# A new opening for a kernel of four transformer layers: fewer rows first, statistics on VectorE, warm-up on a cleared block

## The reference

```python
def rmsnorm(x, g):
    y = xf * lax.rsqrt(jnp.mean(xf * xf, axis=-1, keepdims=True) + RMS_EPS)
    return (y * g.astype(jnp.float32)).astype(x.dtype)

# layer 0, even_mixer
z = rmsnorm(h, mix_norm_g[0]) @ w_in           # w_in: 1024 x 2048
gate_b, gate_c, val, pool_in = z[..., :512], z[..., 512:1024], z[..., 1024:1536], z[..., 1536:]
y_a = gate_b * causal_dwconv(gate_c * val, conv_w)
y_b = multiscale_pool(pool_in, pool_w, pool_scale)
h = h + jnp.concatenate([y_a, y_b], axis=-1) @ w_out
```

## Time and profile before

| what | value |
|---|---|
| median of 3 runs | 1239.06 us (1238.93 to 1239.44) |
| profiled execution | 1239.02 us, its span 1237.3 us |
| TensorE busy | 1222.6 us, 99% of the span |
| VectorE busy | 972.4 us, 79% |
| ScalarE busy | 703.6 us, 57% |
| GpSimd busy | 137.8 us, 11% |
| DMA | 265.78 MB, 215 GB/s on average, 323 GB/s in the first fortieth |

### The profile page before, as it was taken

The page is one execution under the profiler, slowest core; times in us unless marked ns, Lnnn a source line. Parts: engine busy times, 40 slices in busy tenths (PEclk is TensorE's granted clock), DMA queues, the critical chain, the costliest instruction groups (busy, mean ns, idle before and its releaser), DMA issues.

```text
span 1237.3 us, 18561 instructions
## 1 busy us (share of the span) xinstructions
PE 1222.6 (99%) x7005; PEld 1060.6 (86%) x7005; DVE 972.4 (79%) x1232; ACT 703.6 (57%) x1061; POOL 137.8 (11%) x253
## 2 busy tenths in 40 slices
PE   8999999999999999999999999999999999999998
PEld 7989888888778989998889888888878998888887
DVE  5867999977885888898788787997785888676564
ACT  6555555556565655555687566555664353755552
POOL 5000000010001111111132301220010010000000
PEclk9999999999999999999999999999999999999999
DMA  9746777765572798894132348997566488385550
GB/s 323 237 156 211 246 245 237 222 205 183 177 216 69 227 324 312 315 337 128 55 99 93 137 146 294 392 392 259 179 210 216 171 303 273 109 288 195 190 187 34
DMA packets 153777, 265.78 MB, mean 215 GB/s; under 512 B 6220, under 2 KB 110608, under 8 KB 153712
## 3 DMA queue, kind: packets, MB, share of 16 engines
q1 hardware_dynamic: 134560, 204.75, 49.0%
q0 software_dynamic: 18672, 59.67, 13.7%
q10 hardware_dynamic: 480, 0.49, 0.1%
HBM read 263.79 MB, written 1.09 MB: 214 GB/s over the span
## 4 chain that ended last, share of the span: by engine, by line
PE 85%; DVE 9%; ACT 3%; issue 2%; POOL 1%; DMA 1%; ACTq 0%; POOLq 0%; DVEq 0%
PE ps L1969 24%; PE ps L1949 17%; PE ps L1952 9%; PE ps L1935 4%; PE ps L1934 4%; PE ps L1933 4%; DVE w_lo L1150 3%; PE ps L2012 2%; PE ps L2014 2%; PE ps L2013 2%; PE ps L2076 2%; PE ps L1990 2%; PE ps L1992 2%; PE ps L1991 2%; PE ps L2078 2%
## 5 line engine op out<-in xcount | busy, mean ns | idle before, releaser
L1150 DVE TENSOR_TENSOR w_lo<-raw,w_hi 128x2048 fp32r<-128x2048 f32 (+3 forms) x211 | 433.8, 2070 | 31.6 <-ACT w_hi L589 31.3
L589 ACT ACTIVATE w_hi<-raw 128x2048 fp32r<-128x2048 f32 (+3 forms) x213 | 368.7, 1737 | 58.5 <-PE ps L1969 49.2
L1949 PE MATMUL ps<-xn,w_hi 128*128 128x512 f32 x976 | 243.9, 392 | 0.1
L1949 PEld LDWEIGHTS ps<-xn,w_hi 128*128 128x128 f32 x976 | 178.2, 188 | 34.6 <-issue 0.6
L1952 PEld LDWEIGHTS ps<-xn,w_lo 128*128 128x128 f32 x976 | 133.1, 190 | 9.6
L1952 PE MATMUL ps<-xn,w_lo 128*128 128x256 f32 x976 | 136.1, 282 | 0.0
L1969 PE MATMUL ps<-w_hi,a_hi 128*128 128x512 f32 x432 | 134.6, 393 | 0.2 <-DVE a_lo L1874 0.2
L1969 PE MATMUL ps<-w_lo,a_hi 128*128 128x512 f32 x432 | 133.5, 390 | 0.0
L1969 PE MATMUL ps<-w_hi,a_lo 128*128 128x512 f32 x432 | 133.2, 390 | 0.0
L670 ACT ACTIVATE work<-ps 128x512 f32<-128x512 f32 x61 | 36.3, 595 | 168.1 <-PE ps L1952 168.1
L1933 PE MATMUL ps<-xn,w_hi 128*128 128x256 f32 x432 | 122.6, 284 | 0.0
(11 more groups left out here) (370 smaller groups left out, 2006.8 us busy)
## 6 DMA issues: line engine op xcount, KB each, us to landing
raw<-in_ffn_w SPq DMA_DIRECT2D x64, 1024.0 KB, 5.6
side<-in_ada_w POOLq DMA_DIRECT2D x96, 512.0 KB, 6.0
raw<-in_ffn_w_in SPq DMA_DIRECT2D x40, 1024.0 KB, 5.2
raw<-in_ffn_w_out SPq DMA_DIRECT2D x32, 512.0 KB, 5.2
raw<-in_gm_w_in SPq DMA_DIRECT2D x16, 1024.0 KB, 6.0
raw<-in_od_w_in SPq DMA_DIRECT2D x12, 1024.0 KB, 5.6
raw<-in_gm_w_out SPq DMA_DIRECT2D x8, 1024.0 KB, 5.2
raw<-in_ev_w_in SPq DMA_DIRECT2D x7, 1024.0 KB, 12.9
```

The costliest lines, as they stand in the source:

```text
L589: nc.scalar.activation(w_hi[s][:, 0:w], raw[s][:, 0:w], ACT.Copy).then_inc(hi_done, 1)
L1150: nc.vector.tensor_tensor(w_lo[s][:, 0:w], raw[s][:, 0:w], w_hi[s][:, 0:w].bitcast(F32), ALU.subtract)\
L1949: nc.tensor.matmul(o, hi, xn[:, 512 * k:512 * k + 512], start=k == 0, stop=False)
```

## The change

Everything is in the opening, up to the first f tiles.

- Rows: ScalarE's queue loads only the 16 rows of mix_norm_g ahead (`first_rows`). The other 359 rows and the tail of the constants move to SyncE's queue, behind the loads of tiles T_EV to T_EV+3. They are turned after the first f tile, all three groups anew, and VectorE copies them behind the rest of T_EV+3.
- Loads: SyncE loads x's first half, the two parts of T_EV, x's second half, the two parts of T_EV+1, then the others. GpSimd's first side loads wait for `lo_done`.
- Statistics of x's first half: VectorE, with bn_stats and bn_aggr (mean squared plus variance), the power still on GpSimd. The squares of the second half stay with ScalarE, but stand between the second and the third part of the weights. VectorE scales half a row of the second half, GpSimd the other.
- Warm-up: 28 products on a block cleared by GpSimd, before any DMA has landed, then the transpose of the 16 rows, eight products on `ident`, x's transposes, four more products.
- Inputs: ScalarE writes `xn_hi` straight from PSUM, VectorE makes `xn_lo` out of PSUM with one scalar_tensor_tensor for each k. The second half of x is turned into other banks, by fours, ahead of k = 4 and k = 6.
- ScalarE runs one tiny Square first; one semaphore of the conv is merged into another.

```diff
-        first_rows = [x for x in row_pieces if x[0] == 0]
-        later_rows = [x for x in row_pieces if x[0]]
+        first_rows, later_rows = row_pieces[:1], row_pieces[1:]
+        N_FIRST = first_rows[0][2]
...
+        def turned(name, t, b):
+            if name == "ev":
+                c = (b % 2) * P + (S if t and b < 4 else 0)
+                return ps[((2, 3, 5, 6), (2, 3, 4, 7))[t][b // 2]][:, c:c + P]
+            return ps[bank_of(name, t, b // 4)][:, (b % 4) * P:(b % 4) * P + P]
+
+        warm = acc[:, 4, 0:P]
...
+            load_x(0)
+            load_part(T_EV, 0)
+            load_part(T_EV, 1)
+            load_x(1)
+            for m in range(2):
+                load_part(T_EV + 1, m)
+            for t in range(T_EV + 2, T_EV + 4):
+                load(t)
+            for r, p, m, src in later_rows:
+                sp.dma_start(stage[p:p + m, r, :], src).then_inc(in_later, 16)
+            sp.dma_start(cst[:, P:], I["consts"][:, P:C_ALL]).then_inc(in_later, 16)
+            for t in range(T_EV + 4, T_FFN0):
                 load(t)
...
-                    last = gain_op(xf[:, b, t * P:t * P + P], ps[bank_of("ev", t, b // 4)][:, (b % 4) * P:(b % 4) * P + P], ev_gain, None, b)
+                    last = gain_op(xn_hi3[:, b, t * P:t * P + P], turned("ev", t, b), ev_gain, None, b)
...
-            half_squares("ev", 0)
-            half_squares("ev", 1)
+            act.wait_ge(half_ready, 2)
+            nc.scalar.activation(rs[:, 39:40], half[:, 0:1], ACT.Square)
             for i in range(4):
+                if i == 2:
+                    half_squares("ev", 1)
                 split_part(T_EV + i // 2, i % 2)
...
             dve.wait_ge(in_h[0], 16)
+            for c in range(2):
+                last = nc.vector.bn_stats(st[:, 40 + 6 * c:46 + 6 * c], h[:, 0, 512 * c:512 * c + 512])
+            chain(last)
+            chain(nc.vector.bn_aggr(st[:, 4:6], st[:, 40:52]))
+            chain(nc.vector.tensor_scalar(rs[:, 0:1], st[:, 4:5], st[:, 4:5], EPS, ALU.mult, ALU.add))
+            nc.vector.tensor_tensor(rs[:, 0:1], rs[:, 0:1], st[:, 5:6], ALU.add).then_inc(first_stats, 1)
+            dve.wait_ge(vec_ps, 1)
+            nc.vector.tensor_copy(vec[:, 0:N_FIRST], ps[4][:, 0:N_FIRST]).then_inc(vec_ready, 1)
             half_scale("ev", 0)
...
+            def ev_rest(t, i):
+                dve.wait_ge(xf_ready, 4 * t + i + 1)
+                for b in (2 * i, 2 * i + 1):
+                    q = slice(t * P, t * P + P)
+                    last = nc.vector.scalar_tensor_tensor(xn_lo3[:, b, q], turned("ev", t, b), col("mix_norm_g", b),
+                                                          xn_hi3[:, b, q].bitcast(F32), ALU.mult, ALU.subtract)
+                last.then_inc(xn_ready, 1)
+
             for i in range(4):
                 split_part(T_EV + i // 2, i % 2)
-                take("ev", 0, (i,))
-            take("ev", 1)
-            dve.wait_ge(vec_ps, 2)
-            nc.vector.tensor_copy(vec[:, P:N_ROWS], ps[4][:, P:N_ROWS]).then_inc(vec_ready, 1)
+                if i == 2:
+                    dve.wait_ge(rstd_ready, 2)
+                    nc.vector.tensor_scalar(hs[:, 1, 0:512], h[:, 1, 0:512], rstd[:, 1:2], None, ALU.mult).then_inc(hs_ready, 1)
+                ev_rest(0, i)
+            for i in range(4):
+                ev_rest(1, i)
...
             split(T_EV + 2)
             split(T_EV + 3)
+            dve.wait_ge(vec_ps, 2)
+            nc.vector.tensor_copy(vec[:, N_FIRST:N_ROWS], ps[4][:, N_FIRST:N_ROWS]).then_inc(vec_ready, 1)
...
+                            if tt == 0 and name == "ev" and k in (4, 6):
+                                transposes(name, 1, (k // 2 - 2,))
+                            elif tt == 0 and k == 6:
                                 transposes(name, 1)
-                            if name == "ev" and tt == 1 and k == 0:
-                                later_vec_rows()
...
+            pe.wait_ge(half_ready, 2)
+            for _ in range(28):
+                nc.tensor.matmul(ps[7][:, 0:P], warm, warm, start=True, stop=True)
             pe.wait_ge(in_id, 16)
-            for _ in range(11):
+            pe.wait_ge(in_rows, 16)
+            nc.tensor.transpose(ps[4][:, 0:N_FIRST], stage[0:N_FIRST, 0, :], ident[0:N_FIRST, 0:N_FIRST]).then_inc(vec_ps, 1)
+            for _ in range(8):
                 nc.tensor.matmul(ps[7][:, 0:P], ident, ident, start=True, stop=True)
-            pe.wait_ge(in_rows, 16 * len(first_rows))
-            vec_rows(0).then_inc(vec_ps, 1)
             transposes("ev", 0)
-            for _ in range(7):
+            for _ in range(4):
                 nc.tensor.matmul(ps[7][:, 0:P], ident, ident, start=True, stop=True)
...
+            nc.gpsimd.memset(warm, 0.0).then_inc(half_ready, 1)
             nc.gpsimd.memset(half[:, :], -0.5).then_inc(half_ready, 1)
...
+            pool.wait_ge(first_stats, 1)
+            nc.gpsimd.tensor_tensor(rstd[:, 0:1], rs[:, 0:1], half[:, 0:1], ALU.pow).then_inc(rstd_ready, 1)
+            row_rstd("ev", 1)
...
+            pool.wait_ge(hs_ready, 3)
+            nc.gpsimd.tensor_scalar(hs[:, 1, 512:1024], h[:, 1, 512:1024], rstd[:, 1:2], None, ALU.mult).then_inc(hs_ready, 1)
...
+            pool.wait_ge(lo_done, T_EV + 2)
             for s in range(SLOTS):
                 side_load(U_FFN0 + s, ada_view(0, s % 2, s // 2))
```

More of the change, by code:

```diff
@@ L360, in build @@
         in_h = [sem(f"in_h{t}") for t in range(TT)]
[L361 to L364 removed]
+        part_raw, part_hi, part_lo = [sem(f"part_raw{i}") for i in range(2)], sem("part_hi"), sem("part_lo")
+        first_rows, later_rows = row_pieces[:1], row_pieces[1:]
+        N_FIRST = first_rows[0][2]
+        in_id, in_rows = sem("in_id"), sem("in_rows")
         in_later, in_small = sem("in_later"), sem("in_small")
+        first_stats = sem("first_stats")
         vec_ps, vec_ready, cs_ready = sem("vec_ps"), sem("vec_ready"), sem("cs_ready")
@@ L383, in group @@
             return {n: sem(f"{prefix}_{n}") for n in names}
-        EV = group("ev", "gate", "prod", "tap2", "tap1", "conv", "y", "yhi", "a_ready", "pin", "pool", "phi",
+        EV = group("ev", "gate", "prod", "tap2", "conv", "y", "yhi", "a_ready", "pin", "pool", "phi",
                    "pool_ready", "pool_a", "ybf", "ybhi")
@@ L494, in _, with load_x, load_part @@
             x_v = I["x"][0].rearrange("(t p) d -> p t d", p=P)
-            for t in range(TT):
+            def load_x(t):
                 sp.dma_start(h[:, t, :], x_v[:, t, :]).then_inc(in_h[t], 16)
+            def load_part(t, m):
+                full = raw_full[t % SLOTS] if m else part_raw[t - T_EV]
+                dst = raw[t % SLOTS][:, 1024 * m:1024 * m + 1024].rearrange("p (k n) -> p k n", k=2)
+                k = 4 * (t - T_EV) + 2 * m
+                sp.dma_start(dst, kview(ev_w)[:, k:k + 2, 1536:2048]).then_inc(full, 16)
             def load(t):
@@ L672, in split_part @@
             def split_part(t, m):
-                if (t, m) == (T_EV, 0):
-                    act.wait_ge(part_raw, 16)
+                if m == 0:
+                    act.wait_ge(part_raw[t - T_EV], 16)
                 else:
@@ L1336, in _ @@
                 dve.wait_ge(EV["tap2"], 2 * m + 2)
-                for tap, done in ((1, EV["tap1"]), (0, EV["conv"])):
+                for tap in (1, 0):
                     for b in range(2):
@@ L1340, in _ @@
                         nc.vector.scalar_tensor_tensor(av, ev_cv[:, b, tap:tap + S], col("ev_conv_w", 4 * tap + 2 * m + b),
-                                                       av, ALU.mult, ALU.add).then_inc(done, 1)
-                    dve.wait_ge(done, 2 * m + 2)
+                                                       av, ALU.mult, ALU.add).then_inc(EV["conv"], 1)
+                    dve.wait_ge(EV["conv"], 4 * m + 4 - 2 * tap)
                 split(t + 5)
@@ L2033, in norm, with transposes @@
                             last.then_inc(xt_ps, 1)
-            def transposes(name, t):
-                for c in range(2):
+            def transposes(name, t, part=range(2)):
+                for c in part:
                     pe.wait_ge(hs_ready, HS[name] + 2 * t + c + 1)
@@ L2041, in transposes @@
                         b = 4 * c + m
-                        last = nc.tensor.transpose(ps[bank_of(name, t, c)][:, m * P:m * P + P], hs[:, t, b * P:b * P + P], ident)
+                        last = nc.tensor.transpose(turned(name, t, b), hs[:, t, b * P:b * P + P], ident)
                     last.then_inc(xt_ps, 1)
@@ L2648, in row_rstd @@
                     else:
-                        pool.wait_ge(sq_done, sq_count(name, t, 0))
+                        pool.wait_ge(sq_done, 2 if name == "ev" else sq_count(name, t, 0))
                         chain(nc.gpsimd.tensor_scalar(rs[:, c:c + 1], st[:, 2 * t:2 * t + 1], 1.0, EPS, ALU.mult, ALU.add))
```

29 lines of the change are left out of this document (8 added, 21 removed).

## The result

The changed kernel takes 1241.52 us (median of 15 runs, 1240.94 to 1242.45), the kernel before 1238.92 us beside it (15 runs, 1238.69 to 1239.57): ratio 1.0021, 95% interval 1.0014 to 1.0027. The change costs 2.6 us. The forecast was 1241.3. The profiled execution took 1241.83 us with a span of 1240.2, that is 2.8 and 2.9 over those of before. Two disturbed executions (one of x_first_w14 with 1727.29 us, one of the kernel before with 1337.68 us) are in no median of this document.

A forecast was written before the change was run, and what follows sets the result against it. The opening was held bound by a chain of waits back to the first rows, not by TensorE. Terms +0.9 (R), +0.9 (head), +0.35 (rows), +0.1 (Silu) gave +2.3 us on 1239.02: 1241.3 us, range 1237.8 to 1243.0.

The forecast's parts named there:

- R: Start of x's transposes in the opening: forecast 11.6 us against 10.70 before, +0.9 us, set by the longer warm-up.
- Wait for the rows goes: Opening: only 16 rows still awaited, there at about 5.3 us, x's statistics done at 7.5 us, so both inputs early.
- the prediction's formula: End of the 28 warm-up products on TensorE: 1.5 + 6.24 + 0.48c us, 1.5 being TensorE's assumed start.
- c: Length in us of TensorE's first, slow state, 0.427 us per product instead of 0.223; taken as 4.1.
- The head: Stretch from R to the first f tile: end at R + 16.4 against R + 15.5, +0.9 us, TensorE idle before third pair.
- Later rows: After the first f tile: three transposes of the remaining rows and a refill, +0.35 us.
- Silu: ScalarE before the split of T_EV+4: Silu waits for the later rows, +0.1 us if the table load runs ahead.
- (1): Rival: the clock rises late, c = 6.8, TensorE perhaps starting at 1.9: 1242.6 to 1243.0 us; chance 0.13.
- (2): Rival: Silu's table load comes after the wait for the later rows: 1242.6 us; chance 0.08.
- (3): Rival: warm-up products fast from the start or soon, R 9.7 to 10.7: 1239.4 to 1240.3 us; chance 0.20.
- (4): Rival: products fast from the start and TensorE kept fed after R: 1237.0 us; chance 0.17 together with (5).
- (5): Rival: removed wait pays as promised, x sets R near 8.7 us; counted with (4), together 0.17.

The follow-up runs named there:

- x_first_w14: Changed kernel with 14 products on the cleared block, x's second half loaded before the second weight part, its squares and scaling early, Silu later: 1238.69 us, ratio 0.9999.
- silu_later: Changed kernel with Silu and its wait for the later rows moved behind the pool copies and splits of T_EV+4 and T_EV+5: 1242.07 us, ratio 1.0021.
- sq_before_gains: Changed kernel with the squares of x's second half moved between the first split part and the first gains: 1240.43 us, ratio 1.0013.
- w14_short_warmup: Changed kernel with 14 instead of 28 products on the cleared block, nothing else: 1238.78 us, ratio 0.9999.
- order_w14: Changed kernel with 14 products, squares behind the third split, VectorE's half row behind its third inputs, second-half transposes ahead of k = 6, Silu late: 1239.25 us, ratio 1.0002.
- the last two: x_first_w14 with GpSimd's first side loads held until T_EV+4's rest; the second also loads T_EV+4 ahead of 16 small DMAs: 1237.41 and 1236.78 us.
- x_first_side_late: x_first_w14 with GpSimd's first four side loads held until the weight rest of T_EV+4 is made: 1237.41 us, ratio 0.9986.

## Why the prediction was right

It was right by its mechanism: a longer warm-up takes the place of the wait for rows, and the squares' place costs the head as much again. That the number came so close is in part luck: two errors in R cancelled each other, and the median lies nearer to the forecast than the profiled execution, from which the terms are read.

- **Wait for the rows goes**: right. The 16 rows were there by 5.5 (forecast 5.3), rstd at 7.40 (7.5).
- **R, +0.9 forecast, +1.28 measured**: the mis-sized term. TensorE started at 1.16, not 1.5: 0.34 less. The first state lasted 4.9 us, not 4.1, with 22 records at 421 ns up to 6.0 and then 34 at 275: 0.48 x 0.8 = 0.38 more. By the prediction's formula the 28 end at 1.16 + 6.24 + 0.48 x 4.9 = 9.75; the rows' transpose came at 9.93 (0.18 more), the eight at 10.09, and x's transposes 1.89 later (0.11 more than the forecast 1.78). So the early start and the longer first state cancel, and what remains is 0.3 us of handing over between groups of products, which the sum had left out. Three executions with the same opening up to R (the kernel after, silu_later, sq_before_gains) show the rise near 6.06, 4.58 and 4.19 us and R at 11.98, 11.28 and 11.09: 0.7 and 0.89 us for 1.48 and 1.87, a slope of 0.47 to 0.48, as the formula has it. So the profiled execution has a late rise; with c at 3.4, R would be +0.6. The Trainium skill, "TensorE: Matmul & The Clock Gate", says under "What's actually happening" that the number of cold products differs from run to run of one kernel; no row of before could show that, and these three now agree with it.
- **The head, +0.9 forecast, +1.0 measured** (R + 16.51 against R + 15.5). TensorE's wait at the third pair was forecast as over 1 us, released by VectorE, and is 1.41; sq_before_gains takes 1.03 of it away. The pair of input rests takes 0.61 (forecast 0.6).
- **Later rows, +0.35 forecast, +0.32 measured**, with and without the Silu's wait.
- **Silu, +0.1 forecast, +0.15 measured**. The table load did run ahead of its instruction's wait: it stands at 31.11, the wait and Silu behind it at 36.19. Timeline of ScalarE, the kernel after:

```profile
31.11 1.28 ACT L728 ACT_TABLE_LOAD   x1
36.19 0.21 ACT L728 ACTIVATE cs<-vec 128x16 f32<-128x16 f32 x1 [3.80 <-DVE vec L1354]
```

- **The sum**: +2.3 forecast; +2.75 in the profiled execution at the f tiles and +2.8 at the end, +2.6 in the medians. The prediction held that a change under 0.2% can't be told from none; here it can (0.14% to 0.27%), and the measured 0.21% lies over that border, on the side to which the prediction had given 0.35. The profiled execution is 0.5 over the forecast: 0.38 of it in R, 0.1 in the head, 0.05 at the Silu. That the median is lower than the profiled execution fits earlier rises in the other runs, which have no trace; this is argued, not shown.

Of the rivals, (1), the late rise, came about in part: c = 4.9 is over the 4.5 that it named as the point for 0.2%, and the profiled execution is 2.8 us over, though TensorE's early start took back what the late rise had cost. In the two variants with 28 products c was 3.4 and 3.0. The prediction's aside on the granted clock rests on the earlier trace rows, which begin at 26 us; for the opening only the lengths of the records speak, as it goes on to use them. (2) fell by the row at 31.11, (3), (4) and (5) by the 22 records at 421 ns and R. What (4) named, TensorE fed at the third pair and a start before 1.1 us, would probably also have met the DMA wait that x_first_w14 met (argued: no run has just that), and this I had not priced. The "own load has 10 us more" for T_EV+4 held only as long as R was late, and SyncE's 16 issues ahead of it took 9.1 us (8.82 to 17.89), not 7.

What stays open: the changed kernel and its variants scatter more (1240.94 to 1242.45) than the kernel before. The length of the first state, which moves R by half of itself, explains part; but in some executions of the kernels with 14 products (one of w14_short_warmup, five of order_w14, four of x_first_w14, six and three of the last two) 2.3 to 2.9 us lie around the span instead of 1.7, in none of the kernels with 0, 8, 11, 28 or 40, and nothing in a trace says why.

## What to carry to other kernels

A warm-up is paid on the path as soon as what it bridges is there: count its products against the landing of the first real input (here 14 fit, 28 cost 3.8 us of start), and look for the cost at the engine that waits for TensorE, since TensorE itself shows as busy. Work that was free in an idle stretch of ScalarE, such as the squares, costs nearly its full length (here 1.0 of 1.2 us) once moved between two parts that TensorE is waiting for. A head start of 2.8 us didn't show in the median until the loads behind it were put in the order of need: after each gain, read which DMA is late next.

## What the runs showed of the hardware

- From the first product to the change from long records to short ones it took 4.1 us before, 4.9, 3.4 and 3.0 in three executions with 28 products from 1.16 us on, and 6.0 in the one with 40, whose R the formula with that c, and the same 0.3 us between the groups, also gives (15.2); with 8 products, a rest of 1.70 us and eight more, the records were still 421 ns long at the transposes that started at 10.40, and became short near 12.5.
- VectorE and GpSimd slow each other down in the rows where they overlap. GpSimd's half row of 128x512 took 1.57 us when it started 0.24 us ahead of VectorE's 128x1024 rest, and the rest then 1.53 instead of 1.22; it took 2.37 and 2.41 when the rest had started first and stayed at 1.22. VectorE does the same half row in 0.48. Why the first to start has the advantage, no run shows.
- The first of SyncE's small row DMAs took 3.54 us to issue (8.82 to 12.36) behind the 1 MB loads, the others 0.25 to 0.44 each.
- The 16 rows, issued at 1.30, landed 4.2 us later in the kernel after and 5.4 later in x_first_side_late, where TensorE waited 0.60 us for them behind its 14 products, and R was 8.81.
